# Expert value rows gathered by token and summed on TensorE, in place of rows added one by one on VectorE

## The reference

```python
for l in range(DEPTH):                       # DEPTH = 2
    hc = modulate(xc, norm1_g[l], csh1, csc1)
    yc, ctx_states = token_mixer(hc, p, None, (zero_state, zero_state), emit=not last)
    h = modulate(x, norm1_g[l], sh1, sc1)
    y, _ = token_mixer(h, p, rows, ctx_states, emit=True)
    x = x + gt1 * y
    x = x + gt2 * peer(modulate(x, norm2_g[l], sh2, sc2), p)
    if not last:
        xc = xc + cgt1 * yc
        xc = xc + cgt2 * peer(modulate(xc, norm2_g[l], csh2, csc2), p)

def block(hc):                               # peer, hc: 256 tokens x 1024
    ...                                      # scores, two top-16, and the top 16 of their sums, in 8 heads
    u = jnp.take(p['peer_u'], eidx, axis=0)  # eidx: 256 tokens x 8 heads x 16 = 128 slots a token
    act = jax.nn.gelu(jnp.einsum('td,thkd->thk', hc, u), approximate=False) * gw
    v = jnp.take(p['peer_v'], eidx, axis=0)
    return jnp.einsum('thk,thkd->td', act, v)
```

## Time and profile before

| what | value |
|---|---|
| median of 3 runs | 5851.12 us |
| span of the profiled execution, first to last instruction | 5919.7 us |
| busy: PE, DVE, ACT, POOL | 3269.5, 3635.3, 978.0, 1859.8 us |
| read from HBM | 1111.13 MB |
| of it by GpSimd's gathers | 805.40 MB, 1536 gathers |

### The profile page before, as it was taken

The page is one execution under the profiler, slowest core; times in us unless marked ns, Lnnn a source line. Parts: engine busy times, 40 slices in busy tenths (PEclk is TensorE's granted clock), DMA queues, the critical chain, the costliest instruction groups (busy, mean ns, idle before and its releaser), DMA issues. The chain is left out here.

```text
span 5919.7 us, 90317 instructions
## 1 busy us (share of the span) xinstructions
PE 3269.5 (55%) x34182; PEld 2775.1 (47%) x34182; DVE 3635.3 (61%) x7218; ACT 978.0 (17%) x2507; POOL 1859.8 (31%) x1550
## 2 busy tenths in 40 slices
PE   7888776886765005765400288888200000755998
PEld 5677665666654004655400277776100000654777
DVE  3556636668876787688788624654887888133110
ACT  1124211123330001233200012431000000111110
POOL 0000002325543861255577400000378776000000
PEclk9899988887777557877655699998655555866999
DMA  7420045757756983577799633003599998200443
GB/s 268 177 72 3 9 178 210 272 197 231 234 184 231 325 302 111 194 239 240 249 355 356 248 112 100 3 3 97 189 348 324 341 356 296 89 7 25 134 121 121
DMA packets 299022, 1117.25 MB, mean 189 GB/s; under 512 B 33696, under 2 KB 39088, under 8 KB 290224
## 3 DMA queue, kind: packets, MB, share of 16 engines
q0 software_dynamic: 221184, 805.40, 38.7%
q1 hardware_dynamic: 77488, 306.90, 15.2%
HBM read 1111.13 MB, written 1.05 MB: 188 GB/s over the span
## 5 line engine op out<-in xcount | busy, mean ns | idle before, releaser
L1580 POOL DMA_INDIRECT ring<-in_peer_u,expert x496 | 611.3, 1232 | 1332.4 <-DVE expert L1734 734.2
L1862 DVE SCALAR_TENSOR_TENSOR tok<-ring,act,tok 128x1024 f32<-128x1024 f32 x688 | 884.1, 1285 | 130.0 <-DMA ring<-in_peer_v,expert_group 97.8
L161 PE MATMUL psum<-h,weight_ring 128*128 128x256 f32 x3904 | 871.4, 387 | 45.8 <-PEq L87 45.8
L1898 PE MATMUL psum<-constants,tok 128*128 128x128 f32 x48 | 10.2, 403 | 1583.1 <-PEq L87 1583.1
L1814 POOL DMA_INDIRECT ring<-in_peer_v,expert_group x688 | 807.3, 1173 | 226.8 <-issue 212.7
L161 PEld LDWEIGHTS psum<-h,weight_ring 128*128 128x128 f32 x3904 | 758.9, 195 | 157.5 <-issue 49.8
L1898 PEld LDWEIGHTS psum<-constants,tok 128*128 128x128 f32 x48 | 9.4, 219 | 1583.8 <-issue 1583.8
L1560 DVE CUSTOM_DVE_ANT_0 ring<-ring,tok 128x1024 f32<-128x1024 f32 x496 | 597.8, 1221 | 190.1 <-DMA ring<-in_peer_u,expert 169.3
L1814 POOL DMA_INDIRECT ring<-in_peer_u,expert_group x272 | 336.5, 1237 | 662.3 <-DVE expert_group L1850 583.3
L1857 DVE CUSTOM_DVE_ANT_0 ring<-ring,tok 128x1024 f32<-128x1024 f32 x272 | 330.7, 1226 | 80.7 <-DMA ring<-in_peer_u,expert_group 77.0
L1674 PE MATMUL psum<-h,weight_ring 128*128 128x256 f32 x768 | 187.8, 401 | 44.0 <-DMA weight_ring<-in_w_q 29.3
(11 more groups left out here) (532 smaller groups left out, 6492.0 us busy)
## 6 DMA issues: line engine op xcount, KB each, us to landing
weight_ring<-in_w_in SPq DMA_DIRECT2D x228, 512.0 KB
ada_ring<-in_ada_w SPq DMA_DIRECT2D x40, 1024.0 KB, 9.9
weight_ring<-in_w_q SPq DMA_DIRECT2D x48, 512.0 KB
...
```

The costliest lines, as they stand in the source:

```text
L161: mm = pe.matmul(k.bank(slot, tokens), ring[:, slot, j * P:j * P + P], rhs(j), start=(j == 0), stop=(j == w.kt - 1))
L1580: pool.indirect_dma_start(job.ring[:, r % HOSTED, :], None, job.tables[kind], bass.IndirectOffsetOnAxis(ap=job.eidx[:, number:number + 1], ...
L1862: dve.scalar_tensor_tensor(job.tok[:, tile, :], r.ring[:, j, :], r.act8[:, part, j:j + 1], job.tok[:, tile, :], ALU.mult, ALU.add).then_in ...
```

## The change

The u rows stay as they are. A v gather is turned round: it now brings, for **one token**, its 128 slots to the 128 partitions. A **batch** is four such gathers, for four tokens 32 apart (128 rows of 4 KB each: a gather is 512 KB as before), and 64 batches make a job. The sum over the slots is then a multiplication on TensorE: `use_batches` issues eight matmuls of 32 columns of weights by 512 columns of rows, four column strips of the array for each half of the 1024 channels. The weights are a matrix of zeros with one column, `picked`, that GpSimd copies for every batch, so that token c of each strip lands in its own row of PSUM, banks 6 and 7. 32 batches make a tile; `finish_tile` takes the banks out, transposes them and adds them to x. `weigh_tile` makes the weights of one tile as soon as its 128 u rows are used.

```diff
                     multiply(0, slot, True)
-                if rounds > 1:
+                if values_open(k):
+                    use_batches(k, pe, 1)
+                    for i in range(1, rounds):
+                        for slot in range(SLOTS_W):
+                            multiply(i, slot, False)
+                        use_batches(k, pe, 2)
+                elif rounds > 1:
...
         (LdT, TT, TT, TT),
     ]
-    banks = (6, 7, 4, 5)
 
     def product(q, g):
-        return k.bank(banks[(2 * q + g) % 4], 256).rearrange("p (h c) -> p h c", h=4)
+        return k.bank(4 + g)[:, 256 * (q % 2):256 * (q % 2) + 256].rearrange("p (h c) -> p h c", h=4)
 
...
+            if q % 2 or not values_open(k):
+                use_rows(k, dve, 1)
...
                 dve.wait_ge(k.multiplied.sem, k.multiplied.at(lower + i + 1))
                 for turn, (out, mask) in enumerate(((b.Ld, back), (b.LdT, near))):
                     dve.tensor_tensor(out[:, i], pairs(i, turn), masked(mask[ways[i]], 4), ALU.mult).then_inc(k.vec_step.up(), 1)
+                dve.tensor_tensor(b.NT[:, i], pairs(i, 1), masked(far[ways[i]], 4), ALU.mult).then_inc(k.vec_step.up(), 1)
                 marks["ready", i] = k.vec_step.count
-            for i in range(2):
-                dve.tensor_tensor(b.NT[:, i], pairs(i, 1), masked(far[ways[i]], 4), ALU.mult).then_inc(k.vec_step.up(), 1)
-                marks["far", i] = k.vec_step.count
             use_rows(k, dve, 1)
-
...
 
         @block.tensor
         def _(pe):
+            use_batches(k, pe, 1)
...
                             mm = pe.matmul(k.bank(2 * i + 1)[h, at:at + 64], b.TT[h, i, 2 * (c % 2) + j, :], R[h, i, j], start=True, stop=True)
                     mm.then_inc(k.multiplied.up(), 1)
+                use_batches(k, pe, 1)
                 for i in range(2):
...
+                if n == 0:
+                    use_batches(k, pe, 1)
+            if following is None:
+
+                leave_ring(k, pe)
...
+        self.banks = [6, 6]
+
+    def open_batches(self):
+        return BATCHES * min(self.weighed, self.finished + 1 if self.banks[0] == self.banks[1] else 2)
+
+
...
+def use_batches(k, pe, n):
...
-
-
-def expert_weights(k):
+    for m in range(job.batch, min(job.batch + n, job.open_batches())):
+        if m not in job.groups and not value_groups(k):
+            return
+        (tile, c), place = divmod(m, BATCHES), place_batch(k, m)
+
+        for part in place.parts:
+            pe.wait_ge(part.sem, part.landed)
+
+        pe.wait_ge(k.picked.sem, place.picked)
+        for half in range(2):
+            for strip, part in enumerate(place.parts):
+                out = k.bank(job.banks[tile] + half)[STRIP * strip:STRIP * strip + STRIP, :]
+                mm = pe.matmul(out, job.shared.picked[:, m % 2, strip, STRIP - 1 - c:2 * STRIP - 1 - c], part.rows[:, 512 * half:512 * half + 512],
+                               start=(c == 0), stop=(c == BATCHES - 1), skip_group_check=True)
+        mm.then_inc(k.batch_used.up(), 1)
+        for part in place.parts:
+            part.slot.leave(k.batch_used.sem, k.batch_used.count)
...
+def gather_batch(k, pool, m):
+
+
+
+    job, b = k.job, k.job.shared
+    (tile, c), place = divmod(m, BATCHES), place_batch(k, m)
+    if m >= 2:
+
+        pool.wait_ge(k.batch_used.sem, job.consumed[m - 2])
+    if job.weights_kept[tile] is not None:
+        pool.wait_ge(*job.weights_kept[tile])
+    tokens = slice(SLOTS * tile + c, SLOTS * tile + SLOTS, STRIP)
+    pool.tensor_copy(b.picked[:, m % 2, :, STRIP - 1], job.lists.weights[:, tokens]).then_inc(k.picked.sem, 1)
+    for strip, part in enumerate(place.parts):
+        if part.freed is not None:
+
+            pool.wait_ge(*part.freed)
+        token = SLOTS * tile + STRIP * strip + c
+        pool.indirect_dma_start(part.rows, None, b.tables["v"], bass.IndirectOffsetOnAxis(ap=job.lists.turned[:, token:token + 1], axis=0)
+                                ).then_inc(part.sem, 16)
+    job.batches_fetched = m + 1
...
+def fetch_rows(k, pool):
+
 
     job = k.job
-    if job is None or job.weighted or job.row < 2 * SLOTS:
+    if job is None:
         return
-    job.weighted = True
+    rows = range(job.fetched, min(job.row + len(job.shared.slots), 2 * SLOTS))
+    first, last = job.batches_fetched, max(job.batches_fetched, job.batch)
+    ahead = sum(not any(slot.taken for slot in group) for group in value_groups(k))
+    batches = range(first, max(last, min(last + ahead, job.open_batches())))
+    done = 0
+    for n, m in enumerate(batches):
+        upto = len(rows) * (n + 1) // (len(batches) + 1)
+        for r in rows[done:upto]:
+            gather_row(k, pool, r)
+        done = upto
+        gather_batch(k, pool, m)
+    for r in rows[done:]:
+        gather_row(k, pool, r)
+
...
+            act.wait_ge(k.batch_used.sem, job.consumed[BATCHES * (tile + 1) - 1])
+            for half in range(2):
+                act.activation(b.y[:, 512 * half:512 * half + 512], k.bank(bank + half), ACT.Copy).then_inc(k.act_step.up(), 1)
+                marks[half] = k.act_step.count
+
+        @block.tensor
...
                         score(n - 1)
+                    use_batches(k, pe, 1)
...
+                use_batches(k, pe, 10)
+                k.groups = []
...
+def finish_experts(k, job, then=None):
...
     with ExitStack() as inner:
-        r = buffers(k, inner, ring=[RING, 1024], dot8=[2, RING], act8=[2, RING])
-        idx8 = [inner.enter_context(k.sbuf("expert_group", [RING], U32)) for _ in range(2)]
-        groups = SLOTS // RING
-        rounds = groups // 2
+        spare = buffers(k, inner, spare=[12, 1024]).spare
+        own = b.slots
+        extra = [Slot(spare[:, j, :], k.gathered[8 + j]) for j in range(12)]
+        b.slots, job.turn = [*own, *extra[0:4]], 4
...
+                    job.weights_kept[tile] = k.act_step.sem, k.act_step.count
+
+            @block.tensor
+            def _(pe):
+                for n, tile in enumerate(todo):
+                    if tile == 1 and job.weighed == 0:
+                        job.weighed = 1
+                        use_batches(k, pe, 1)
+
+                    pe.wait_ge(k.vec_step.sem, k.vec_step.at(n + 1))
+                    pe.transpose(k.bank(2 + tile, SLOTS), b.dots[:, tile, :], k.ident).then_inc(k.turned.up(), 1)
+                job.weighed = 2
+                use_batches(k, pe, 2 * BATCHES)
 
...
-HOSTED_CONTEXT, HOSTED_FIRST, HOSTED_LAST = 336, 240, 0
```

523 lines of the change are left out of this document (297 added, 226 removed).

## The result

The changed kernel is slower: 5963.02 us (median of 4 runs, 5955.67 to 5973.59) against 5853.29 for the kernel before (4 runs, 5850.55 to 5863.13), a ratio of 1.0173 with a 95% interval of 1.0149 to 1.0197. The forecast was 5725. The profiled execution of the changed kernel has a span of 5971.7 us, 52 over the 5919.7 from which the prediction was made, though the runs differ by 110. Its extra 56 us are spread over the recurrences and finishes, so the table's picture of where the time went stands, with those stages some 10 us each too favourable to the change.

The account below looks back on a forecast made before the run. Finishes were taken as bound by gathers on DMA, hosted recurrences nearest VectorE's limit. Terms -269 + 72 + 47 + 20 - 16 + 20 = -126 us off a 5919.7 span, scaled to run time, gave 5725 us; range 5595 to 5845.

Parts of the forecast that it names:

- Steps 1 and 2: Context's finish falls from 340 to 71 us (-269); the choice, taking in 104 gathers, grows by 72 to 185.
- Step 3: Recurrence units hosting batches get 6 us longer (bounds -5 to +14): +47 in the x mixer, +20 in the context mixer.
- Usable 8.3 us after the batch before was used: In recurrence units, four gathers into just-freed buffers are ready after 0.4 + 3 x 1.25 + 4.2 = 8.3 us.
- Less the inversion, 4.5: In a unit, the inversion loses 7 of 14 VectorE rows: 8.4 us if all on the path, taken as 4.5.
- Rival B: In units TensorE waits in line on the single buffer group; a unit grows 43 us, span 6055; chance 0.11.
- The multiplications and the norm behind the recurrence: Behind the x mixer's recurrence, multiplications lose 28 v rows on VectorE and gain four batches: 0 us.
- Step 4: Inversion products alternate in halves of one packed PSUM bank: no new wait, 0 to 6 us, taken as 0.
- Step 5: Finish of x in layer 0: 415 us against 431 (-16); last finish: 812 against 792 (+20).
- rival C: In finishes two batches in flight are too few: a v row takes 1.75 us, total 5855, no change; chance 0.10.
- lower bound of 1.39 for the v gather: In the finishes a v gather takes 1.52 us, at best 1.39, its time at 378 GB/s.
- VectorE's relief is worth nothing in a finish: Finishes go by gathers, DMA share 0.94 to 0.96, not by VectorE; only moving gathers into slack stretches wins time.
- Rival A: Batches' waits hide: units 5 us shorter, v rows at 1.42, the choice at 175, total 5570; chance 0.22.

Follow-up runs that it names:

- E1: Changed kernel, but TensorE does not wait for hosted batches' gathers (multiplications read the token tile, value sums left out): 5832.44 us, ratio 0.9942.
- E3: Changed kernel with no batches in the recurrence's units and the inversion's 14 u rows restored: 5969.14 us, ratio 1.017.
- E6: E5 plus a second group of buffers in the norm and bonus stages behind the recurrence: 5756.23 us, ratio 0.9809.
- E5: E4 with the batch that ended a unit's first chunk step moved into the inversion: 5755.72 us, ratio 0.9801.
- E12: E11 plus a second group of buffers in the two stages behind the recurrence: 5648.41 us, ratio 0.9623.
- E11: Changed kernel with E3 and E4 combined, no batches in units and four buffer groups in finishes: 5678.62 us, ratio 0.968.
- E4: Changed kernel with four groups of buffers in the finishes instead of two, and four buffers for picked: 5744.57 us, ratio 0.9796.
- E7: E4 with three groups of buffers in the finishes in place of four: 5752.34 us, ratio 0.9807.
- E9: E5 with GpSimd's part of the inversion written behind TensorE's, so the refill follows three u rows instead of nine: 5890.62 us, ratio 0.9967.
- E8: The kernel before, unchanged, run once more for a second profile: span 5863.7 us.

## Why the prediction was wrong, step by step

**Steps 1 and 2, context's finish and choice: right in sum.** Predicted 71 + 185 = 256 from the mixer's end, measured 267. DMA carries 328 GB/s in the choice's first 99 us (339 to 378 had been taken), and TensorE waits 18 us there for the batches' rows.

**Step 3, the units: wrong, and the main cause.** Predicted +6 a unit, measured +19 to +22 (58 to 61, now 80). The two recurrences took 116 us more than forecast, which uses up nearly all of the 126 that the change was to gain; with the next point the sign turns. What failed is the wait in front of a batch, put at about 7 us of TensorE's time a unit and measured at 29.4. By its own parts:
- "Usable 8.3 us after the batch before was used": it is 11.0. The 4.2 us from issue to use were read from a single row on an idle queue; behind three gathers it is 6.6. Three exposed turns: 8 us.
- "1.8" for the multiplications: 1.92 only for the first, 3.64, 3.64 and 3.29 for the three that follow a wait, at the lower clock. I had both prices and took the high clock for a stretch in which TensorE now stands still before every batch. 5 us.
- The second batch's gathers should have begun right at the release; the u rows ahead of them held them 5 us, so that the wait is 13.2 against the 5.6 that VectorE had caused there.
- "Less the inversion, 4.5": no run has this alone. E1's units, with 7 rows fewer and nothing waited for, are 5.4 us longer than E3's (65.5 against 60.1), where four batches at 1.92 less 4.5 would make it 3.2. So the relief may have been smaller; it is not shown.

Rival B described this ("u rows between, which wait for VectorE, which waits for TensorE"), gave twice what came (43 a unit), and named its own threshold: 3.5 us more per hosted batch than reckoned. Over the 36 batches, the 116 us of the recurrences make 3.2, just under it, and with the 26 behind the first recurrence 3.9. It was given 0.11. The listings of the change could have told more: every link of the ring stands in them, and with a single group of buffers its turn is a serial chain whatever else is slack.

**The multiplications and the norm behind the recurrence were put at 0: wrong.** They grew by 30 us. Pairs of batches stand back to back there with one group between them, and the second waits 10.99, 9.83 and 9.99 us (at 1910.62, 1948.26 and 1995.01). A second group there took 11 us back (E6, 66 us against 77 of E5), and 22 where no batches stand in the units (E12 against E11).

**Step 4, packed banks: right.** 735.2 us against 735.4 with nothing hosted.

**Step 5, finishes: right in sum for a wrong reason.** Last finish 812 predicted, 814 measured. But a v row took 1.74, not 1.52, which is rival C (1.75), and a u row 1.35, not 1.56. E4 and E7 show that two batches in flight were too few. The prediction's case against C, that two batches are the eight rows that the ring held, failed on this: of 300 us of v rows GpSimd waited 86 for TensorE to release a batch.

```profile
POOL picked L1724 <- PE psum L1693: 85.9, 31, 4.3
```

The reading under both, that DMA with a share of 0.94 to 0.96 is full at 1.48 us a row, was wrong: E4 moves a row in 1.26 to 1.30. The lower bound of 1.39 for the v gather was therefore no bound, and the largest thing to be had in this kernel was not seen. What set the pace in the finishes of before was GpSimd. This is its view of waits in the first profile of before, over the 360 us of v rows:

```profile
POOL ring L1814 <- issue: 75.7, 241, 2.6
POOL ring L1814 <- DVE tok L1862: 3.2, 1, 3.2
```

Its busy time of 281 us and these 79 fill the window, and only 3.2 of them are a wait for a buffer, so more buffers alone would not have helped before. A row took the gather's own time and some 0.3: 1.16 + 0.3 for v, and for u 290/231 = 1.25 + 0.3, the 1.56 of the earlier trace rows. That own time depends on VectorE. Where VectorE does nothing, in the v rows of the changed kernel, of E4 and of E9, every one of 172, 238 and 207 gathers takes 0.93 to 0.97 us, also in E9, where DMA was slower. Beside VectorE's rows, in the finishes of before, of the changed kernel and of E4, the means are 1.00 to 1.29, the longest 1.99. So taking the multiply-add away did shorten a v row, from 1.48 (1.41 in E8) to the 1.26 of E4, and "VectorE's relief is worth nothing in a finish" was wrong; in the changed kernel the two groups hid it. The Trainium skill (SBUF — State Buffer, "SBUF: two separate sides") has GpSimd locked out of the port through which it writes descriptors while VectorE runs a copy in a two-port mode. The prediction set it aside because DMA's share was 0.96 already, and that argument fails with the reading of the share. The longer gathers beside VectorE go the way of the rule; that the multiply-add and the multiply and sum take the port like such a copy is not shown by any run here.

**Rival A** (waits hide, units at 53 to 56) had 0.22 and nothing for it came true, though its finish at 1.42 was nearer than mine to what E4 shows to be possible.

Still open: why u rows sped up from 1.56 to 1.35 us with the change. All of it is the gather's own time on GpSimd, 1.25 and now 1.05 (1.00 in E4, 1.10 in E5), beside the same VectorE instruction of 1.22 us and with the same number of buffers; what differs is that the loop is written out and the copies of numbers in groups of eight are gone. No run separates these.
